# Token lists of experts 1 to 15 by indirect transfers of 8-byte pairs in place of one-hot products

## The chip, the cores and the metric

The kernel runs on one core of one Trainium2 chip. The core has a matrix engine (TensorE, PE in the profile), a vector engine (VectorE, DVE), a scalar engine (ScalarE, ACT), a general engine (GpSimd, POOL) and a queue engine for transfers (SyncE, SP); each runs its own list of instructions and meets the others at semaphores. 16 DMA engines move data between the chip's memory (DRAM) and the core's memories, SBUF (128 partitions) and PSUM (eight banks that TensorE writes to). The metric is the device time of one execution in microseconds (us), the median of several runs.

## What is computed

One layer of an encoder for 2064 tokens (16 learned ones and 2048 of the input) of 1024 channels: a pooling mixer, then a mixture of 16 experts in which each expert picks its 258 tokens itself, then a norm. The part that matters here is the choice of tokens:

```
cap = CAPACITY_FACTOR * T // N_EXPERTS                      # 258
logits = jnp.einsum('btd,de->bte', u, router_w).astype(jnp.float32)
aff = jax.nn.softmax(logits, axis=-1)
g, idx = lax.top_k(jnp.swapaxes(aff, 1, 2), cap)
...
xs = ub[ib]                                                 # the 258 rows of each expert
hid = silu(xs @ w_gate) * (xs @ w_up)
ys = (hid @ w_down) * g
out = zeros((T, D)).at[ib].add(ys)
```

All is float32. Each expert has three weight matrices of 1024 x 2048, 8 MB each.

## The kernel before

**Stages.** First the mixer and the router's logits, 19 tiles of up to 128 tokens (`step` on each engine). Then a search finds, for all experts at once, the affinity that lets 258 tokens pass. `find_slots` turns the choice into a place from 0 to 257 for each chosen token, in the layout of the tokens: partition and tile (`slot`, 128 x 16 experts x 19 tiles); tokens that were not chosen get a place far outside. It runs for expert 0 first, and for experts 1 to 15 after expert 0's list has been read.

**The expert loop.** For each expert `gate_up` makes the hidden values in 32 quarters and `down` the result in 16. A quarter is 24 matmuls of 128 x 128 by 258 columns: each weight block is split into a high and a low part (`w_hi` by ScalarE, `w_lo` by VectorE in `split_rest`), and so are the tokens and the hidden values, and three products of the parts are added for each of 8 blocks. The splits run three quarters ahead of TensorE. SyncE loads pieces of 1 MB into the four slots of `raw`, each as soon as its slot has been split.

**The token list.** A list is needed in another layout than the places are in: place 0 to 127 down the partitions, 128 to 255 likewise, and the last two tokens each repeated for eight chunks of channels. It holds for each place the token's number and its affinity. For the list of expert n+1, made while expert n runs, VectorE compares each of 19 tiles' places (and one empty tile) with the row of all places (`pick`, five tiles in each of the four turns of `gate_up`, L940), which gives one-hot matrices of 128 x 272. Between gate/up and down TensorE multiplies these with `vals`: token number in two parts and affinity in three, all bfloat16 and exact in sum (`make_list`, L1156; three blocks of 19 matmuls of 5 columns, 57 in all). At the first down quarter VectorE copies the finished expert's indices aside (`idx_now`, `gates_now`, `idx_small`) and puts the new list together (`read_list`, L943).

**What follows a list.** GpSimd waits for it (`list_v`), and gathers the 258 rows with three indirect transfers (`gather`, L484) into `x_rows` and `x_left`. TensorE transposes them from the eighth down quarter on. After the expert's end GpSimd adds the weighted results to `h_acc` in DRAM by three indirect transfers (L527 to L531). `carry_wait` is a tiny multiplication on GpSimd that lets the transfers behind it start only after the waits before it.

## Time and profile before

| | |
|---|---|
| median of 3 runs | 2591.71 us (2591.68 to 2593.68) |
| the profiled execution | 2591.47 us |
| its span, first to last instruction | 2589.4 us |
| busy in the span: PE, DVE, ACT, POOL | 96%, 54%, 46%, 7% |
| mean busy share of the 16 DMA engines in the expert loop | 0.60 |
| mixer, router and first list | 0 to 256 us |
| experts | 256 us to the end, some 145 us each |

A row of the timeline gives the start of an instruction, its length, its engine and line, what it writes and reads, and in brackets how long the engine stood idle before it and what released it. Matmuls overlap: each takes about 0.28 us from its start to its end, and the next may start 0.12 us after it. What a matmul adds to the time is the distance between starts. "xN" after a row counts instructions that were merged into it. "issue" in place of a releaser means that the engine waited for nothing that the profile shows.

### The profile page before, as it was taken

How to read it: one execution, taken by the hardware profiler on the slowest of the kernel's cores; microseconds unless marked ns; L12 is line 12 of the kernel's file. 1: busy time of each engine (PE TensorE's matmuls, PEld its weight loads, DVE VectorE, ACT ScalarE, POOL GpSimd, SP SyncE). 2: the span in 40 equal slices, each digit the busy share in tenths (PEclk: the TensorE clock that was granted, in tenths of full speed). 3: DMA queues.
4: the chain of work that ended last, by engine and by line, in shares of the span. 5: the costliest groups of instructions: out<-in, count | busy, mean ns of one | idle time of the engine just before them, and what ended most of it. 6: DMA issues, size and time to landing. Idle time of an engine off the chain costs nothing.

```text
span 2589.4 us, 55918 instructions
## 1 busy us (share of the span) xinstructions
PE 2475.4 (96%) x21150; PEld 2462.9 (95%) x21150; DVE 1397.3 (54%) x2161; ACT 1192.6 (46%) x1765; POOL 193.3 (7%) x190
## 2 busy tenths in 40 slices
PE   7962999999999999999999999999999999999996
PEld 7952999999999999999999999999999999999996
DVE  5556555546454555555454655555454555555474
ACT  5630444444444444444444444444444445444454
POOL 0020001010100001010101001010101001010101
PEclk9975999999999999999999999999999999999998
DMA  7640556665655656565655666666656656566694
GB/s 218 199 147 19 167 194 190 195 178 191 191 185 179 194 195 192 197 178 194 180 188 185 193 194 179 201 184 198 179 179 192 196 186 187 195 181 205 217 316 168
DMA packets 426299, 485.83 MB, mean 188 GB/s; under 512 B 11537, under 2 KB 406529, under 8 KB 426274
## 3 DMA queue, kind: packets, MB, share of 16 engines
q1 hardware_dynamic: 411106, 433.85, 52.4%
q0 software_dynamic: 10560, 34.87, 5.4%
q10 hardware_dynamic: 4608, 16.78, 1.7%
q8 instruction: 16, 0.26, 0.0%
q14 instruction: 9, 0.07, 0.0%
HBM read 443.26 MB, written 42.21 MB: 187 GB/s over the span
## 4 chain that ended last, share of the span: by engine, by line
PE 95%; DVE 2%; issue 1%; DMA 1%; ACT 0%; DVEq 0%; POOL 0%; SPq 0%; POOLq 0%; ACTq 0%
PE bank L1069 92%; PE bank L1074 3%; DVE above L875 0%; DVE above_b L875 0%; DMA nmix<-in_norm_mix 0%; DVE base L882 0%; DMA x_left<-u_rows,idx_chunk 0%; ACT u_t L623 0%; DVE picks L940 0%; DVE pooled_lo L791 0%; DVE pw L818 0%; DVE flips L878 0%; DVE y_rows L1061 0%; ACT junk L719 0%; ACT squares L593 0%
## 5 line engine op out<-in xcount | busy, mean ns | idle before, releaser
L963 DVE TENSOR_TENSOR w_lo<-raw,w_hi 128x1024 fp32r<-128x1024 f32 x765 | 930.1, 1222 | 526.1 <-ACT w_hi L654 524.9
L1069 PE MATMUL bank<-x_hi,w_hi 128*128 128x258 f32 x4096 | 1163.1, 284 | 5.8 <-issue 3.9
L1069 PE MATMUL bank<-x_lo,w_hi 128*128 128x258 f32 x4096 | 1157.5, 283 | 0.0
L1069 PE MATMUL bank<-x_hi,w_lo 128*128 128x258 f32 x4096 | 1153.5, 282 | 0.0
L654 ACT ACTIVATE w_hi<-raw 128x1024 fp32r<-128x1024 f32 x765 | 804.7, 1052 | 271.4 <-PE bank L1069 234.0
L1069 PEld LDWEIGHTS bank<-x_hi,w_hi 128*128 128x128 f32 x4096 | 771.0, 188 | 10.3 <-issue 10.3
L1069 PEld LDWEIGHTS bank<-x_lo,w_hi 128*128 128x128 f32 x4096 | 777.2, 190 | 0.0
L1069 PEld LDWEIGHTS bank<-x_hi,w_lo 128*128 128x128 f32 x4096 | 773.0, 189 | 0.0
L1069 PE MATMUL bank<-hid_hi,w_hi 128*128 128x258 f32 x2048 | 586.6, 286 | 0.0
L1069 PE MATMUL bank<-hid_lo,w_hi 128*128 128x258 f32 x2048 | 579.8, 283 | 0.0
L1069 PE MATMUL bank<-hid_hi,w_lo 128*128 128x258 f32 x2048 | 579.4, 283 | 0.0
L1069 PEld LDWEIGHTS bank<-hid_lo,w_hi 128*128 128x128 f32 x2048 | 388.0, 189 | 0.0
L1069 PEld LDWEIGHTS bank<-hid_hi,w_lo 128*128 128x128 f32 x2048 | 387.3, 189 | 0.0
L1069 PEld LDWEIGHTS bank<-hid_hi,w_hi 128*128 128x128 f32 x2048 | 386.7, 189 | 0.6 <-DVE w_lo L963 0.2
L992 DVE TENSOR_TENSOR hid<-silu,bank 128x258 f32<-128x258 f32 x256 | 108.6, 424 | 505.1 <-PE bank L1069 505.1
L708 ACT ACTIVATE hid_hi<-hid 128x258 f32 (+1 forms) x256 | 107.8, 421 | 458.6 <-DVE hid L992 456.6
L704 ACT ACTIVATE silu<-bank 128x258 f32<-128x258 f32 x256 | 98.9, 386 | 289.0 <-PE bank L1069 289.0
L481 POOL TENSOR_TENSOR carrier<-carrier 128x1 f32<-128x1 f32 x30 | 5.8, 192 | 2003.7 <-DVE gates L958 1338.3
L732 ACT ACTIVATE y_t<-bank 128x258 f32<-128x258 f32 x128 | 49.5, 386 | 201.7 <-PE bank L1069 201.7
L998 DVE TENSOR_TENSOR hid_lo<-hid,hid_hi 128x258 f32 (+1 forms) x256 | 107.8, 421 | 0.0
L940 DVE TENSOR_SCALAR picks<-iota,slot 128x272 bf16 (+1 forms) x320 | 81.8, 288 | 3.3
L528 POOL DMA_INDIRECT h_acc<-y_rows,idx_now x30 | 74.9, 2496 | 12.5 <-issue 12.5
(143 smaller groups left out, 1208.9 us busy)
## 6 DMA issues: line engine op xcount, KB each, us to landing
raw<-in_moe_w_gate SPq DMA_DIRECT2D x128, 1024.0 KB, 5.2
raw<-in_moe_w_up SPq DMA_DIRECT2D x128, 1024.0 KB
raw<-in_moe_w_down SPq DMA_DIRECT2D x128, 1024.0 KB, 4.9
h_in<-in_x SPq DMA_DIRECT2D x18, 512.0 KB, 5.7
x_rows<-h_acc ACTq DMA_DIRECT2D x16, 512.0 KB, 6.0
out<-x_rows ACTq DMA_DIRECT2D x16, 512.0 KB, 4.3
h_acc<-h_mid SPq DMA_DIRECT2D x17, 448.0 KB, 4.9
u_rows<-u_out SPq DMA_DIRECT2D x17, 448.0 KB, 3.0
```

Source lines behind the costliest of these rows:

```text
L481: nc.gpsimd.tensor_tensor(carrier[:, 0:1], carrier[:, 1:2], carrier[:, 1:2], ALU.mult)\
L528: pool.indirect_dma_start(h_acc, bass.IndirectOffsetOnAxis(ap=idx_now[:, b:b + 1], axis=0), y_rows[:, b, :], None, compute_op=ALU.add).the ...
L654: nc.scalar.activation(w_hi[:, a % 4], quarter_view(piece % 4, a % 2), ACT.Copy)\
L704: nc.scalar.activation(silu[:, fc], bank[:, q % 4, 0:CAP], ACT.Silu)\
L708: nc.scalar.activation(hid_hi[:, ds(4 * b + fc, 1)], hid[:, fc % 2:fc % 2 + 1], ACT.Copy).then_inc(hid_hi_done, 1)
L732: nc.scalar.activation(y_t[:, m], bank[:, m % 4, 0:CAP], ACT.Copy).then_inc(y_t_done, 1)
L940: nc.vector.tensor_scalar(picks[:, ds(c0 + c, 1), :], iota[:].unsqueeze(1), src, None, ALU.is_equal).then_inc(picks_done, 1)
L963: nc.vector.tensor_tensor(w_lo[:, a % 4], quarter_view(a // 2 % 4, a % 2), w_hi[:, a % 4].bitcast(f32), ALU.subtract).then_inc(split_lo, 1)
L992: nc.vector.tensor_tensor(hid[:, fc % 2], silu[:, fc], bank[:, q % 4, 0:CAP], ALU.mult).then_inc(hid_done, 1)
L998: nc.vector.tensor_tensor(hid_lo[:, col], hid[:, fc % 2:fc % 2 + 1], hid_hi[:, col].bitcast(f32), ALU.subtract)\
L1069: return nc.tensor.matmul(dst, lhs, rhs, start=start, stop=stop)
L1074: return nc.tensor.matmul(dst, src, ident[0:n, 0:n], is_transpose=True, start=True, stop=True)
```

## The change

Expert 0's list is made as before (`pick`, `make_first_list`, `read_first_list`, now for this expert alone). For the others the one-hot matrices, `pick` in `gate_up` and `make_list` in TensorE's loop are gone, and so are the waits that went with them. In their place:

- `find_slots` for experts 1 to 15 writes places as integers (`slot_rows`); a token that was not chosen gets 4096 plus its partition (`far`, one more column that is loaded at the start). GpSimd keeps a copy of the affinities, turned by expert (`aff_kept`).
- `send_list(n)`, on GpSimd at the head of its loop for expert n, makes the list of expert n+1: it copies the expert's places and affinities aside, issues 19 indirect transfers of 128 pairs (token number, affinity; 8 bytes) to the row `place` of a table of 258 rows in DRAM, where a place over 257 is out of bounds and leaves nothing, waits until all have landed, and reads the table back in the layout of the list by three transfers.
- `read_list` on VectorE waits for that (`list_read`) and makes `idx`, `idx_chunk` and `gates` by three instructions instead of six.

```diff
+            def send_list(n):
+
+                pool.wait_ge(list_copied, 2 * n + 1)
+                nc.gpsimd.tensor_copy(slot_now[:], slot_rows[:, ds(n + 1, 1), :].rearrange("p a c -> p (a c)"))\
+                  .then_inc(list_copied, 1)
+                nc.gpsimd.tensor_copy(pair_now[:, :, 1].bitcast(f32),
+                                      aff_kept[:, ds(n + 1, 1), :].rearrange("p a c -> p (a c)"))\
+                  .then_inc(list_copied, 1)
+                pool.wait_ge(list_copied, 2 * n + 3)
+                pool.wait_ge(carrier_set, 4 * n + 1)
+                carry_wait()
+                for c in range(NT):
+                    pool.indirect_dma_start(list_rows, bass.IndirectOffsetOnAxis(ap=slot_now[:, c:c + 1], axis=0),
+                                            pair_now[:, c, :], None, bounds_check=CAP - 1, oob_is_err=False)\
+                        .then_inc(list_sent, 16)
+                pool.wait_ge(list_sent, 16 * NT * n + 16 * NT)
+                pool.wait_ge(carrier_set, 4 * n + 2)
+                carry_wait()
+                with nc.allow_non_contiguous_dma(reason="a list of pairs"):
+                    pool.dma_start(listed_rows[:, 0:2, :], list_rows[0:256, :].rearrange("(b p) v -> p b v", p=P))\
+                        .then_inc(list_read, 16)
+                    for t in range(LEFT):
+                        pool.dma_start(listed_rows[t:SMALL_ROWS:LEFT, 2, :],
+                                       list_rows[256 + t].partition_broadcast(KD)).then_inc(list_read, 16)
...
             gather()
+            pool.wait_ge(slotted, 1)
+            pool.wait_ge(aff_saved, 1)
             with pool.Fori(0, NE - 1) as n:
-                pool.wait_ge(list_v, LV * n + 2 * LV)
-                pool.wait_ge(carrier_set, 2 * n + 1)
+                send_list(n)
+                pool.wait_ge(list_ready, 3 * n + 6)
+                pool.wait_ge(carrier_set, 4 * n + 3)
                 pool.wait_ge(x_turned, XT * n + XT)
                 carry_wait()
                 gather()
...
+            def read_list(m):
+
+                dve.wait_ge(list_kept, 3 * m)
+                dve.wait_ge(list_read, 16 * READS * m)
+                dve.wait_ge(gathered, 48 * m)
+                nc.vector.tensor_copy(idx[:], listed_rows[:, :, 0]).then_inc(list_ready, 1)
+                nc.vector.scalar_tensor_tensor(out=idx_chunk[:], in0=listed_rows[:, 2, 0:1], scalar=float(KD),
+                                               in1=chunk[:], op0=ALU.mult, op1=ALU.add).then_inc(list_ready, 1)
+                nc.vector.tensor_copy(gates[:], listed_rows[:, :, 1].bitcast(f32)).then_inc(list_ready, 1)
...
-                    if q == 3 and not last:
-                        dve.wait_ge(listed_ps, n + 1)
-                        pick(n + 1, 5 * b)
...
             with pe.Fori(0, NE - 1) as n:
                 with pe.Fori(0, 4) as b:
                     gate_up(n, b)
-                make_list(n + 1, n + 1)
                 for q in range(16):
                     down_quarter(n, q)
```

The order of the instructions on the engines shows where these stand. TensorE at the end of gate/up in the expert loop, before: the last of the 57 small matmuls, and the first down quarter behind them.

```order
L1069 MATMUL bank<-vals,picks 128x5
L1069 ISA
L1069 MATMUL bank<-vals,picks 128x5 x20
L1069 MATMUL bank<-vals,picks 16x5 x19
L1215 ISA
L1216 ISA [waits split_lo]
L1219 REGISTER_ALU [waits hid_lo_done]
L1069 MATMUL bank<-hid_hi,w_hi 128x258 [waits silu_done]
```

The same place after the change:

```order
L1132 MATMUL bank<-x_hi,w_lo 128x258
L1294 REGISTER_ALU
L1294 COMPARE_AND_BRANCH
L1274 ISA
L1275 ISA [waits split_lo]
L1278 REGISTER_ALU [waits hid_lo_done]
L1132 MATMUL bank<-hid_hi,w_hi 128x258 [waits silu_done]
```

The down quarter now follows the last gate/up quarter directly, with the waits that it had. GpSimd at the head of its expert loop, before:

```order
L516 UNCONDITIONAL_BRANCH
L516 ISA
L518 ISA [waits list_v]
L519 ISA [waits carrier_set]
L481 TENSOR_TENSOR carrier<-carrier 128x1 [waits x_turned]
L486 DMA x_rows<-u_rows,idx 128x1024 x2
L489 DMA x_left<-u_rows,idx_chunk 16x128
```

and after the change, from behind the two copies of `send_list` to the carrier ahead of the same gather:

```order
L540 ISA [waits list_copied]
L501 TENSOR_TENSOR carrier<-carrier 128x1 [waits carrier_set]
L543 DMA list_rows<-pair_now,slot_now 258x2 x19
L546 ISA
L547 REGISTER_ALU [waits list_sent]
L501 TENSOR_TENSOR carrier<-carrier 128x1 [waits carrier_set]
L550 DMA listed_rows<-list_rows 128x2x2
L553 DMA listed_rows<-list_rows 8x2 x2
L566 ISA
L567 REGISTER_ALU [waits list_ready]
L568 ISA [waits carrier_set]
L501 TENSOR_TENSOR carrier<-carrier 128x1 [waits x_turned]
```

22 transfers and two waits for transfers now stand ahead of GpSimd's wait for the list. VectorE at the first down quarter, where the list is read, before:

```order
L945 REGISTER_ALU
L946 COPY listed<-bank 128x10 [waits listed_ps]
L948 COPY listed<-bank 16x5
L949 ISA
L950 TENSOR_TENSOR part<-listed 128x3 [waits list_v]
L951 REGISTER_ALU
L952 SCALAR_TENSOR_TENSOR idx<-listed 128x3 [waits gathered]
L955 REGISTER_ALU
L956 SCALAR_TENSOR_TENSOR idx_chunk<-idx,chunk 128x1 [waits list_v]
L958 TENSOR_TENSOR gates<-part,listed 128x3
L962 REGISTER_ALU
L963 TENSOR_TENSOR w_lo<-raw,w_hi 128x1024 [waits split_hi]
```

and after:

```order
L1018 ISA
L1019 REGISTER_ALU [waits list_kept]
L1021 COPY idx<-listed_rows 128x3 [waits gathered,list_read]
L1022 SCALAR_TENSOR_TENSOR idx_chunk<-listed_rows,chunk 128x1
L1024 COPY gates<-listed_rows 128x3
L1028 REGISTER_ALU
L1029 TENSOR_TENSOR w_lo<-raw,w_hi 128x1024 [waits split_hi]
```

The wait for TensorE's product (`listed_ps`) became a wait for transfers (`list_read`), and the same weight split stands behind it.

## Rows read from the trace of the kernel before

**Rows 1.** The page: busy us, share of the span and instructions of each engine.

```profile
PE 2475.4 (96%) x21150; PEld 2462.9 (95%) x21150; DVE 1397.3 (54%) x2161; ACT 1192.6 (46%) x1765; POOL 193.3 (7%) x190
```

**Rows 2.** The page: the chain that ended last, shares of the span by engine.

```profile
PE 95%; DVE 2%; issue 1%; DMA 1%; ACT 0%; DVEq 0%; POOL 0%; SPq 0%; POOLq 0%; ACTq 0%
```

**Rows 3.** Stretches: length, busy us (count) of PE, PEld, DVE, ACT, POOL; clock, DMA, GB/s.

```profile
1000.00:2000.00 1000.00, 998.05 (x8601) 994.94 (x8600) 533.12 (x792) 466.02 (x678) 68.27 (x55) 1.00 0.60 188
```

**Rows 4.** PE's waits by line waited for: us in total, times, longest us.

```profile
PE bank L1074 <- DMA x_left<-u_rows,idx_chunk: 8.8, 1, 8.8
...
PE bank L1069 <- issue: 3.9, 14, 0.3
```

**Rows 5.** Timeline of PE, from gate/up to down of expert 0: start, us, line.

```profile
350.93 1.93 PE L1069 MATMUL bank<-vals,picks 128*128 x57
352.79 0.39 PE L1069 MATMUL bank<-hid_hi,w_hi 128*128 128x258 f32 x1
353.01 0.28 PE L1069 MATMUL bank<-hid_lo,w_hi 128*128 128x258 f32 x1
353.13 0.28 PE L1069 MATMUL bank<-hid_hi,w_lo 128*128 128x258 f32 x1
```

**Rows 6.** The fifteen lists' matmuls on `picks`, summed over fifteen stretches of 10 us.

```profile
sum 150.00, PE 28.91 PEld 26.23 DVE 0.00; mean PE 1.93 PEld 1.75 DVE 0.00
```

**Rows 7.** Timeline of DVE around its first list reading in the loop.

```profile
352.69 0.42 DVE L998 TENSOR_TENSOR hid_lo<-hid,hid_hi 128x258 f32 x1
...
354.54 0.16 DVE L946 COPY listed<-bank 128x10 f32<-128x10 f32 x1
...
355.17 0.15 DVE L958 TENSOR_TENSOR gates<-part,listed 128x3 f32<-128x3 f32 x1
```

**Rows 8.** Timeline of POOL, experts 0 and 1.

```profile
355.59 0.19 POOL L481 TENSOR_TENSOR carrier<-carrier 128x1 f32<-128x1 f32 x1 [108.74 <-DVE gates L958]
...
357.56 1.57 POOL L486 DMA_INDIRECT x_rows<-u_rows,idx  x1 [0.30 <-issue]
...
405.40 2.65 POOL L528 DMA_INDIRECT h_acc<-y_rows,idx_now  x1 [0.53 <-issue]
...
410.99 1.33 POOL L530 DMA_INDIRECT h_acc<-y_small,idx_small  x1 [0.30 <-issue]
500.14 0.19 POOL L481 TENSOR_TENSOR carrier<-carrier 128x1 f32<-128x1 f32 x1 [87.82 <-DVE gates L958]
```

**Rows 9.** The last, bounded scatter (L571): ns min/median/max, starts; and its landing.

```profile
L571 POOL DMA_INDIRECT out<-y_rows,idx_out x3: 893/981/1170, 2575.5 to 2578.3; - x3
...
DMA to landing us min/median/max: 2.5/3.5/3.5
```

**Rows 10.** DMA queues: packets, MB, share of 16 engines; one issue with us to landing.

```profile
q1 hardware_dynamic: 411106, 433.85, 52.4%
q0 software_dynamic: 10560, 34.87, 5.4%
...
h_acc<-y_rows,idx_now POOLq DMA_INDIRECT x30, 9.2
```

**Rows 11.** Timeline of SP, two loads into one slot; and landing of all gate/up pieces.

```profile
414.22 0.37 SPq L440 DMA_DIRECT2D raw<-in_moe_w_gate  x1
...
437.23 0.37 SPq L440 DMA_DIRECT2D raw<-in_moe_w_gate  x1
...
DMA to landing us min/median/max: 5.1/5.2/8.1
```

**Rows 12.** Timelines of the start and of the end of `find_slots` for experts 1 to 15.

```profile
21.34 0.29 POOL L472 CAST tri_b<-cst 128x128 bf16<-128x128 f32 x1 [18.24 <-DMA nfin<-in_norm_final]
...
25.33 1.21 DVE L810 TENSOR_TENSOR h_mid<-bank,h_in 128x1024 f32<-128x1024 f32 x1
...
247.98 0.45 DVE L930 TENSOR_SCALAR slot<-place 128x285 f32<-128x285 f32 x1
```

**Rows 13.** DVE's weight splits in one expert: count, ns min/median/max, starts.

```profile
L963 DVE TENSOR_TENSOR w_lo<-raw,w_hi x33: 1217/1220/1227, 405.3 to 497.7; 128x1024 fp32r<-128x1024 f32 x33
```

More of the change, by code:

```diff
@@ L112, in constants @@
     put("tok_lo", tok % 16)
+    put("tok", tok)
+    put("far", FAR + k)
     low = 4.0 ** np.arange(PAIRS - 1, -1, -1)
@@ L156, in encoder_kernel @@
         iota = sb("iota", [P, PICKED], bf16)
-        slot = sb("slot", [P, NE, 20], f32)
-        vals = sb("vals", [P, NE, 20, 5], bf16)
+        slot = sb("slot", [P, 20], f32)
+        vals = sb("vals", [P, 20, 5], bf16)
+        slot_rows = sb("slot_rows", [P, NE, NT], i32)
+        aff_kept = sb("aff_kept", [P, NE, NT], f32)
+        slot_now = sb("slot_now", [P, NT], i32)
+        pair_now = sb("pair_now", [P, NT, 2], i32)
+        listed_rows = sb("listed_rows", [P, 3, 2], i32)
+        far = sb("far", [P, 1], f32)
         listed = sb("listed", [P, 3, 5], f32)
@@ L392, in _ @@
                 sp.dma_start(chunk[:], consts[:, cols["chunk"][0]:cols["chunk"][1]]).then_inc(loaded_c, 16)
+            with nc.allow_non_contiguous_dma(reason="a column"):
+                sp.dma_start(far[:], consts[:, cols["far"][0]:cols["far"][1]]).then_inc(loaded_c, 16)
             sp.dma_start(reset[:], consts[:, cols["reset"][0]:cols["reset"][1]]).then_inc(loaded_c, 16)
@@ L1165, in make_list @@
                     for c in range(NT):
[L1166 removed]
+                        if b == 0 and c % 5 == 0:
                             pe.wait_ge(picks_done, c + 5)
[L1168 to L1169 removed]
+                        last = mm(bank[0:n, 6, 5 * b:5 * b + 5], picks[:, c, s0:s0 + n], vals[:, c, :],
+                                  c == 0, c == NT - 1)
                 last.then_inc(listed_ps, 1)
             def turn_pair(i, m):
[L1174 to L1175 removed]
+                if i == 2 and isinstance(m, int):
+                    pe.wait_ge(list_v, 2)
                 for k in (2 * i, 2 * i + 1):
```

96 lines of the change are left out of this document (52 added, 44 removed).

## The prediction

> **What bounds the kernel now.** I read the page's table of busy time first: TensorE is busy 96% of the span, VectorE 54%, ScalarE 46% and GpSimd 7% [rows 1]. A busy share alone says little for pipelined matmuls, so next the chain that ended last: TensorE holds 95% of it [rows 2]. Then the stretches: from 1000 to 2000 us TensorE is busy 998.05 of 1000 us at a granted clock of 1.00, while the DMA engines are at 0.60 [rows 3]. Last TensorE's waits: in the fifteen experts it waits for nobody. What that view names lies in the router and at the first list, but for the fourteen loop edges between experts, 0.3 us each [rows 4]. So in the expert loop the time is the sum of TensorE's steps. What is taken out of that sum is gained in full, and what other engines do costs nothing until TensorE begins to wait.
>
> **The change part by part.**
>
> *TensorE, removed.* Between the last gate/up quarter and the first down quarter of each of 15 experts stand 57 matmuls of `make_list`. Their busy time, 28.91 us summed over 15 windows [rows 6], counts the overlap with the following step, so I take start to start: 350.93 to 352.79, 1.86 us, and the same at all experts, since the sum is 15 times 1.93. The first down step after them takes 0.22 (352.79 to 353.01), where the next takes 0.12 [rows 5]. Inside the gate/up stage there is no such long step at a quarter's edge, so I book the extra 0.10 as a consequence of the small matmuls too. Per expert 1.96 us, for 15 experts 29.4 us; without the 0.10 it is 27.9. I take 29.4, since the quarters on the two sides are of one kind, and keep 27.9 for the range.
>
> Does anything become late when the down stage starts 1.96 us earlier? Its first two quarters need weights that VectorE has long split. Its third begins 2 x 24 x 0.12 = 5.76 us after 350.93, at 356.7, and needs all of hid_lo, which ends at 352.69 + 0.42 = 353.1 [rows 5, 7]. So no wait takes the place of the matmuls.
>
> *VectorE, removed.* 20 comparisons in each of 15 experts, and half of the list's reading (six small instructions become three). VectorE waits for ScalarE and TensorE in that stage and TensorE never for it, so this is worth nothing.
>
> *GpSimd, added.* For each list: two small copies, two carriers, 19 indirect transfers, a wait until they landed, three plain transfers that read the list back. All of it lies on an engine that idles 87.82 us at a stretch [rows 8], and is hidden if the list is in SBUF when VectorE asks. The budget: GpSimd is free at 410.99 + 1.33 = 412.3. VectorE's next list reading starts 0.8 us before 500.14 (354.54 to 355.32 is its length) [rows 7, 8], and 1.96 earlier after the change: 497.4. That leaves 85.1 us. VectorE then has some patience: behind the reading stands the split for the fifth down quarter, which begins at 350.93 + 4 x 2.88 = 362.4; less 1.22 for the split and 0.8 for the reading the list may come at 360.4, 5.9 us after VectorE asked at 354.5. Together 91.0 us.
>
> The need, between the cheapest and the dearest rows of the same kind. An indirect transfer of 128 rows costs GpSimd 0.89 when it is a bounded scatter to DRAM [rows 9], 1.57 for a gather and 2.65 for a scatter that adds [rows 8], and 0.30 to the next: 19 x 1.19 = 22.6 to 19 x 2.95 = 56.1 us. Landing takes 2.5 [rows 9] to 9.2 us [rows 10], and once more for the reading. The three plain transfers have no row; as 1.19 to 2.95 each they are 3.6 to 8.9. Copies and carriers I take as four times a carrier with its gap, 0.19 + 0.53 [rows 8]: 2.9. Sum: 34 to 86 us. I take about 40, since the bounded scatter is the same form of instruction. Even the dear end fits into 91.0. The first list has more room: its slots are ready at 247.98 + 0.45 = 248.4 [rows 12] and VectorE asks at 354.5.
>
> Who is queued behind it: on GpSimd only the gather of the same expert, which needs the list anyway; the scatter-add of the finished expert comes later still. On VectorE the weight splits stand behind the new wait for `list_read`, which is where a late list would reach TensorE.
>
> *DMA, added.* Up to 19 x 128 = 2432 packets of 8 bytes per list, of which 258 are in bounds; whether the others move anything no row shows. The weights' queue takes 52.4% of 16 engines' span for 411106 packets, 53 ns each; the software queue 5.4% for 10560, 212 ns each [rows 10]. So a list costs 0 (dropped) to 8 us at the one price and 32 us at the other, of all 16 engines, within some 143 us that leave 40% free [rows 3]. A weight slot is loaded every 437.23 - 414.22 = 23.0 us; less two quarters of reading, 5.8, there are 17.2 us from issue to need, against a landing of 5.2, at most 8.1 [rows 11]. Slack 9 to 12 us. If the queues take turns, the weights get half of the engines where they need 0.60, for at most 64 us: 6 us behind, inside the slack. I take nothing.
>
> *The start.* One more small load (`far`) delays the constants by about 0.5 us; they are in by 21.3, and VectorE first waits for them after the instruction at 25.33 [rows 12]. Nothing. Shorter fills of `vals` lie under the threshold search. Nothing.
>
> *The sum.* Profiled execution 2591.47 us (span 2589.4 and 2.07 around it); less 29.4 is 2562.1. The median of the three runs, 2591.71, stands 0.24 above the profiled one, well within what is left open here.
>
> **A rule that speaks against it.** What the rows show: VectorE's splits run at 1217 to 1227 ns in the expert where GpSimd issues its scatter-adds [rows 13], and the gather at 357.56 took 1.57 beside a split [rows 8]. The Trainium skill, SBUF — State Buffer, under "A bandwidth-pool intuition that's wrong", says that a DMA issued from GpSimd takes about 620 ns alone and about 3100 ns beside a VectorE copy, since GpSimd can't write its descriptors while VectorE holds the port that the two share. By that figure the sum would be an estimate of 19 x 3.4 = 65 us, some 4 us too late with all else at the dear end, and the time about 2615. The same page, under "Who interferes with whom", has an operation on two SBUF tensors, as the split is, take only the read side of that port; the rows above agree in that neither engine is stretched fivefold. Rival 1 has the same mechanism at the prices of rows.
>
> **The rivals.**
>
> *1. The list is late (slower).* Place: VectorE's wait for `list_read` at the first down quarter. It decides from (91.0 - 30.2) / 19 = 3.2 us per transfer, gap included, if all the rest is dear (2.9 + 9.2 + 8.9 + 9.2 = 30.2), and from 4.2 if it is cheap (11.5). Price, with the dearest row and a whole split of 1.22 in front of each: 2.65 + 1.22 + 0.30 = 4.17, 79.2 + 30.2 = 109.4, 18.4 late in 14 experts: 258 us, time 2820. For it: no row has 19 such transfers in a row. Against it: the bounded scatter at 0.89 to 1.17.
>
> *2. Weight pieces are late.* If the small packets go ahead of the weights rather than in turn with them, a part of 32 us falls on one slot. One us beyond the slack per expert gives 15 back: 2577. For it: the software queue's 212 ns per packet; against it: those are packets of kilobytes.
>
> *3. The change doesn't do what it says.* If the small matmuls only filled a wait, the first down quarter would start when hid_lo is done, at 353.1, and the time would stay 2591. Against it: the first down quarter needs only the first eight of the sixteen, and the third quarter starts after 353.1 by itself.
>
> **How the numbers follow.** Forecast 2562.1 with 84%; its own range 2560 to 2565, from 27.9 at one end and a little more than 29.4 at the other. Rival 1: 8%, of which 3 are for GpSimd being held behind VectorE. Rival 2: 5%, from 2566 to 2600, mostly below. Rival 3: 3%. A measurement of this kernel can tell about 0.2%, 5 us, from no change. Faster by more than that: 84 and most of rival 2, 87%. Within it: 5%. Slower: 8%. The range 2559 to 2570 holds the forecast with its bounds and the small end of rival 2.
>
> **What would show it.** TensorE's matmuls on `vals` and `picks` are left at the first list alone, and a down stage follows gate/up with a step of 0.12. The period of an expert, by GpSimd's carriers 500.14 - 355.59 = 144.55 [rows 8], falls to 142.6. GpSimd shows 19 transfers at 0.9 to 1.6 us and then idles until VectorE's gates are set: if instead VectorE's first list copy waits for a DMA, rival 1 holds. ScalarE waits for `raw` DMAs: rival 2. What would make the prediction wrong altogether is a cost of TensorE's own, such as another granted clock than 1.00 in the loop, for which no row gives a reason.

## The result, and the profile after

The changed kernel takes 2761.57 us (median of 4 runs, 2759.86 to 2764.64) against 2591.69 for the kernel before in the same session: 1.066 times as long, 95% interval 1.064 to 1.067. The forecast was 2562.1, a gain; the kernel got slower, and lies 199 us over the forecast. Its profiled execution spans 2759.3 us.

The list was not late, the weights were not late, and TensorE did lose the small matmuls. The first three views, in the order of the prediction, already show where the time went. The page's busy times (us, share of the span, instructions), which answer to [rows 1]:

```profile
PE 2539.8 (92%) x20295; PEld 2498.7 (91%) x20295; DVE 1330.5 (48%) x1816; ACT 1191.7 (43%) x1765; POOL 549.0 (20%) x583
```

TensorE has 855 matmuls fewer (15 x 57) and is yet busy for longer. The stretch of [rows 3], and three shorter ones of the expert that starts at about 557 us (length, busy us and counts of PE, PEld, DVE, ACT, POOL; granted clock, DMA share, GB/s):

```profile
1000.00:2000.00 1000.00, 942.25 (x7461) 926.54 (x7459) 453.85 (x573) 423.80 (x619) 225.30 (x225) 0.95 0.56 171
555.00:574.00 19.00, 18.75 (x159) 18.47 (x158) 8.48 (x11) 10.29 (x16) 13.19 (x12) 1.00 0.75 188
576.00:595.00 19.00, 8.91 (x32) 6.93 (x33) 0.15 (x1) 1.33 (x2) 13.81 (x16) 0.59 0.11 29
601.00:640.00 39.00, 39.00 (x326) 39.00 (x325) 19.97 (x25) 18.39 (x27) 0.00 (x0) 1.00 0.59 189
```

From 576 to 595 TensorE does 32 matmuls where 159 fit; VectorE does one instruction, ScalarE two, the DMA engines rest, and GpSimd alone works. The granted clock, 1.00 on both sides, is 0.59 in between: TensorE's pauses begin at 576, and by 580 the clock is at its lower level (1.2 of 2.4 GHz), where it stays to the end of the pauses and nearly until 600. Three pieces of two us:

```profile
576.00:578.00 2.00, 1.03 (x7) 0.94 (x8) 0.00 (x0) 0.00 (x0) 1.52 (x2) 1.00 0.37 110
...
580.00:582.00 2.00, 1.33 (x5) 1.24 (x6) 0.00 (x0) 0.81 (x2) 1.39 (x3) 0.50 0.02 1
...
600.00:602.00 2.00, 2.00 (x19) 2.00 (x18) 0.42 (x2) 1.33 (x2) 0.00 (x0) 1.00 0.82 261
```

The stretch falls into the one in which GpSimd sends the list: the first of the list's transfers starts at 567.40, the last ends at 591.96 and has landed by 593.2, and TensorE's pauses run from 576 to 594.7. GpSimd's timeline (start, length, line; the idle time before and what ended it), first the list sent during expert 1, then the one during expert 2:

```profile
425.62 1.07 POOL L543 DMA_INDIRECT list_rows<-pair_now,slot_now  x1 [0.15 <-issue]
427.00 2.07 POOL L543 DMA_INDIRECT list_rows<-pair_now,slot_now  x1 [0.30 <-issue]
429.37 1.30 POOL L543 DMA_INDIRECT list_rows<-pair_now,slot_now  x1 [0.30 <-issue]
430.98 1.85 POOL L543 DMA_INDIRECT list_rows<-pair_now,slot_now  x1 [0.30 <-issue]
...
455.96 0.99 POOL L543 DMA_INDIRECT list_rows<-pair_now,slot_now  x1 [0.30 <-issue]
...
461.28 1.07 POOL L553 DMA_DIRECT2D listed_rows<-list_rows  x2
510.67 1.02 POOL L501 TENSOR_TENSOR carrier<-carrier 128x1 f32<-128x1 f32 x1 [48.33 <-DVE gates L1024]
...
567.40 1.06 POOL L543 DMA_INDIRECT list_rows<-pair_now,slot_now  x1 [0.15 <-issue]
568.77 1.01 POOL L543 DMA_INDIRECT list_rows<-pair_now,slot_now  x1 [0.30 <-issue]
...
589.70 0.98 POOL L543 DMA_INDIRECT list_rows<-pair_now,slot_now  x1 [0.30 <-issue]
590.98 0.98 POOL L543 DMA_INDIRECT list_rows<-pair_now,slot_now  x1 [0.30 <-issue]
```

Both lists are early: in expert 1 GpSimd then idles 48.33 us until VectorE has read it. What differs is the length of the transfers. In expert 1 ten of the nineteen take 1.26 to 2.07 us, each of them beside one of VectorE's splits, and nothing is lost: its period is 141.8 us, 2.8 under that of the kernel before. In expert 2 all take 0.98 to 1.17 and follow each other 1.28 to 1.47 apart, and TensorE stops. (In this kernel no transfer that is clear of VectorE's work takes over 1.07 us. Not every one beside a split is stretched: the one at 568.77 is not.) Experts 1 and 4 are of the first kind, the other thirteen of the second. Measured from its first matmul to the first of what follows, the gate/up stage takes 91.42 us in experts 1 and 4 (92.16 before) and 106.7 to 110.0 in the others.

What TensorE waits for there. Its waits (us in total, times, longest), answering to [rows 4], where this was 3.9 us:

```profile
PE bank L1132 <- issue: 109.4, 170, 1.8
```

and a piece of its timeline in expert 2, matmuls first, then weight loads:

```profile
586.55 0.42 PE L1132 MATMUL bank<-x_hi,w_lo 128*128 128x258 f32 x1
586.89 0.38 PE L1132 MATMUL bank<-x_hi,w_hi 128*128 128x258 f32 x1
589.00 0.37 PE L1132 MATMUL bank<-x_lo,w_hi 128*128 128x258 f32 x1 [1.74 <-issue]
```

```profile
586.55 0.34 PEld L1132 LDWEIGHTS bank<-x_hi,w_hi 128*128 128x128 f32 x1
588.29 0.29 PEld L1132 LDWEIGHTS bank<-x_lo,w_hi 128*128 128x128 f32 x1 [1.40 <-issue]
```

"issue" means that nothing in the trace released it. These matmuls are in the middle of a quarter, where the program has no wait, and the weight load itself comes late, so it is not a matmul that waits for its weights. One to four matmuls come, then 0.3 to 2.1 us pass to the start of the next, about one group per GpSimd transfer. ScalarE and VectorE stand still too. ACT's timeline, the last matmul of TensorE's seventh quarter, and DVE's timeline:

```profile
571.81 0.39 ACT L753 ACTIVATE silu<-bank 128x258 f32<-128x258 f32 x1 [1.47 <-PE bank L1132]
...
581.19 0.39 ACT L753 ACTIVATE silu<-bank 128x258 f32<-128x258 f32 x1 [8.05 <-issue]
```

```profile
579.02 0.28 PE L1132 MATMUL bank<-x_hi,w_lo 128*128 128x258 f32 x1 [0.79 <-issue]
```

```profile
573.18 1.22 DVE L1029 TENSOR_TENSOR w_lo<-raw,w_hi 128x1024 fp32r<-128x1024 f32 x1 [1.58 <-issue]
594.85 0.42 DVE L1058 TENSOR_TENSOR hid<-silu,bank 128x258 f32<-128x258 f32 x1 [20.45 <-remote]
595.19 1.22 DVE L1029 TENSOR_TENSOR w_lo<-raw,w_hi 128x1024 fp32r<-128x1024 f32 x1
```

ScalarE's second `silu` of that turn follows the first after one quarter, 2.85 us, when nothing is wrong; that would be 574.7, ahead of TensorE's first pause (576), and it starts at 581.19. This looks as if ScalarE stopped by itself, and first. It did not: `silu` and `hid` wait for TensorE's count of finished quarters (the semaphore `quarters`), and that count comes late. The last matmul of the seventh quarter starts at 579.02, and TensorE goes on with the eighth; the `hid` that needs the seventh starts at 594.85. "remote" means that a semaphore moved then although no instruction of this trace ended; "issue" at 581.19 means here that the event is not on record, as the trace has only 30 of the 32 counts of this expert's gate/up stage. In the kernel before, each count comes 0.3 us after the start of the quarter's last matmul. In e2 below, whose trace has every count, the latest comes 8.4 to 12.8 us after it in each of thirteen experts, and every `silu` of these starts within 0.15 us of its count, as before the change. As the ends of matmuls are modelled, the trace does not tell whether the quarter itself ended late or only its count was late.

The late count costs TensorE time by itself. Its tenth quarter needs the split at 595.19, which stands behind that `hid`; undisturbed the quarter would start at 556.6 + 9 x 2.86 = 582.3. So some 14 of the 18.6 us that this expert loses would be lost even if TensorE did not pause. While VectorE waits, its splits do not hold GpSimd back either: the transfers stay at their shortest until the list is out.

The sum agrees: the excess of the gate/up stages over 91.42 us is 200 us in twelve experts, and 12 in expert 0 over its stage in the kernel before (94.9); 212 in all, and 2761.6 - 212 = 2549, which is what the first experiment gives. The view of waits names 109 us of it; the rest is matmuls that start 0.21 us apart at the lower clock (589.17 to 589.38) in place of 0.12, and pauses that this view counts short or not at all.

### The profile page after: what moved, and what is told of

Read it like the earlier page. It is cut to its first block, busy times and chain, and to the rows that moved or that the text cites. A ratio compares the mean times of both kernels' runs of the same rounds, so it can differ in the third digit from the quotient of the medians.

```text
span 2759.3 us, 53642 instructions
## 1 busy us (share of the span) xinstructions
PE 2539.8 (92%) x20295; PEld 2498.7 (91%) x20295; DVE 1330.5 (48%) x1816; ACT 1191.7 (43%) x1765; POOL 549.0 (20%) x583
## 3 DMA queue, kind: packets, MB, share of 16 engines
q0 software_dynamic: 21120, 35.08, 5.3%
## 4 chain that ended last, share of the span: by engine, by line
PE 92%; issue 5%; DVE 2%; ACT 0%; DMA 0%; DVEq 0%; POOL 0%; SPq 0%; ACTq 0%; POOLq 0%
PE bank L1132 89%; PE bank L1137 3%; DVE above L924 0%; DVE above_b L924 0%; DMA nmix<-in_norm_mix 0%; DVE base L931 0%; DMA x_left<-u_rows,idx_chunk 0%; ACT u_t L672 0%; DVE picks L995 0%; DVE pooled_lo L840 0%; DVE pw L867 0%; DVE flips L927 0%; DVE y_rows L1124 0%; ACT junk L768 0%; ACT squares L642 0%
## 5 line engine op out<-in xcount | busy, mean ns | idle before, releaser
L1132 PE MATMUL bank<-x_lo,w_hi 128*128 128x258 f32 x4096 | 1182.0, 289 | 45.9 <-issue 44.9
L1132 PE MATMUL bank<-x_hi,w_hi 128*128 128x258 f32 x4096 | 1182.3, 289 | 38.6 <-issue 35.3
L1132 PE MATMUL bank<-x_hi,w_lo 128*128 128x258 f32 x4096 | 1181.2, 288 | 30.4 <-issue 29.2
L1132 PEld LDWEIGHTS bank<-x_lo,w_hi 128*128 128x128 f32 x4096 | 794.7, 194 | 56.7 <-issue 56.0
L1132 PEld LDWEIGHTS bank<-x_hi,w_lo 128*128 128x128 f32 x4096 | 796.2, 194 | 48.5 <-issue 48.2
L1132 PEld LDWEIGHTS bank<-x_hi,w_hi 128*128 128x128 f32 x4096 | 795.0, 194 | 45.3 <-issue 44.6
L501 POOL TENSOR_TENSOR carrier<-carrier 128x1 f32<-128x1 f32 x60 | 37.5, 625 | 1723.2 <-DVE gates L1024 1058.8
L543 POOL DMA_INDIRECT list_rows<-pair_now,slot_now x285 | 305.6, 1072 | 85.7 <-issue 84.1
```

The source lines that it names most:

```text
L501: nc.gpsimd.tensor_tensor(carrier[:, 0:1], carrier[:, 1:2], carrier[:, 1:2], ALU.mult)\
L543: pool.indirect_dma_start(list_rows, bass.IndirectOffsetOnAxis(ap=slot_now[:, c:c + 1], axis=0), pair_now[:, c, :], None, bounds_check=CAP ...
L1132: return nc.tensor.matmul(dst, lhs, rhs, start=start, stop=stop)
```

## Experiments

**Theory:** indirect transfers that GpSimd sends back to back stop the other engines; the expectations say "starve", since I took the engines to be left without instructions. **Rivals:** TensorE's own changed program (shorter loop, tiles at other bytes); the reading back; the small writes in DRAM; a GpSimd that is merely busy; the backward branch of TensorE's gate/up loop; the place of the transfers in the expert.

The diffs below are cut to the lines that carry the change, without declarations, waits and semaphore counts; where runs share a block, a comment names the run. Stages and lists are measured in each run's profiled execution.

### e1: the list sent once

```diff
+            fill_table(0)
             with pool.Fori(0, NE - 1) as n:
                 send_list(n)
```

`fill_table` is the two copies and the 19 transfers, taken out of `send_list`, which keeps the carriers, the wait and the three reading transfers.

> The changed kernel, but the 19 transfers of a list are sent once, ahead of the expert loop; every expert from 1 on reads back that one list of expert 1 (its output is therefore that of a kernel that routes 14 experts alike). The three plain GpSimd transfers that read the list back, the waits and both programs of TensorE and VectorE are as in the changed kernel. Theory (the run of GpSimd's transfers starves TensorE): the 13 disturbed experts become like experts 1 and 4, whose period is 141.8 us; 2591.5 - 15 x 2.8 = 2549 us, 2545 to 2556. Rival (TensorE's own program, its shorter loop or the new tile addresses, does it): near 2760. Rival (the reading back does it): near 2760 too, with the stand-still of TensorE at the reading back alone.

2549.23 us, ratio 0.984 (0.983 to 0.986). TensorE's pauses are gone, but for four of 1.7 us in all beside the one list that is sent, ahead of the loop:

```profile
PE bank L1136 <- issue: 5.2, 18, 0.7
```

TensorE's program, the tiles' places and the reading back are those of the changed kernel, so these rivals fall. It is also what the change would bring without its side effect.

### e2, e10, e11, e12, e15: what it is in the transfers

All five are the kernel before, with all its work, and something added to GpSimd at the place where the changed kernel sends its list.

```diff
             with pool.Fori(0, NE - 1) as n:
+                for c in range(NT):      # e2; e10: spot[0:64], pair[0:64]
+                    pool.indirect_dma_start(spare_rows, IndirectOffsetOnAxis(ap=spot[:, c:c + 1], axis=0),
+                                            pair[:], None, bounds_check=NT * P - 1, oob_is_err=False)
+                for c in range(26):      # e11
+                    nc.gpsimd.tensor_tensor(busy_out[:], busy_in[:], busy_in[:], ALU.mult)
+                for c in range(NT):      # e12
+                    pool.dma_start(spare_rows[c * P:(c + 1) * P, :], pair[:])
+                for c in range(NT):      # e15
+                    pool.indirect_dma_start(fetched[:, c, :], None, spare_rows,
+                                            IndirectOffsetOnAxis(ap=spot[:, c:c + 1], axis=0))
```

> The kernel before, all of its work kept, and on GpSimd at the place where the changed kernel sends a list 19 indirect transfers per expert to a spare table, every index out of bounds, so that no pair is written. Theory (the run of GpSimd's transfers starves TensorE, whatever they carry): some 13 of 15 experts get 15 to 19 us longer, 2591.5 + about 200 = 2750 to 2850. Rival (the 258 small writes of a list in DRAM do it): 2591, within 5. Rival (TensorE's changed program does it): 2591, within 5.

> The kernel of e2 with 64 indices per transfer in place of 128, all out of bounds. Undisturbed it is 2592 + 15 = 2607, since gate/up quarters take 2.91 at this place of x_hi. Theory A (what each transfer writes into its queue fills it, so half the rows are half the load): no stand-still, 2600 to 2615. Theory B (the number of transfers per time, not their rows): 15 stand-stills as in e2, 2780 to 2830.

> The kernel before with 26 GpSimd multiplications of 128x304 numbers per expert at the place of e2's transfers, about 1 us each, some 26 us in all, and no transfer. Theory (the transfers do it): no stand-still; 2607 by the place of x_hi, 2600 to 2620, with something more where GpSimd and VectorE stretch each other. Rival (a GpSimd that is busy without a break does it): 15 stand-stills, 2750 or more.

> The kernel of e2 with 19 plain GpSimd transfers of 128 pairs of 8 bytes to a spare table, at addresses known to the program, in place of the indirect ones; all pairs are written. Undisturbed 2607. Theory A (a dense run of GpSimd transfers of any kind does it): stand-stills in most experts, 2700 or more. Theory B (only indirect transfers, which read indices and make each row's address on the fly): 2600 to 2615.

> The kernel before with 19 indirect gathers of 128 pairs of 8 bytes from a spare table into SBUF per expert, at the place of e2's transfers, in place of scatters to it. Undisturbed 2607. Theory (any indirect GpSimd transfer, issued back to back, starves TensorE): as e2, 2700 to 2850. Rival (the scatter form with its bound, whose indices are compared, does it): 2600 to 2615.

Measured: e2 2816.65 us (ratio 1.085 to 1.088), e10 2850.40 (1.098 to 1.102), e15 2833.51 (1.090 to 1.097): in each TensorE stops in all fifteen experts. e11 2605.03 (1.003 to 1.007) and e12 2604.57 (1.003 to 1.006): no pause, and no more than the 2607 that the place of `x_hi` accounts for. TensorE's waits on "issue", in the order e2, e10, e15, e11, e12:

```profile
PE bank L1093 <- issue: 104.1, 205, 2.2
```

```profile
PE bank L1093 <- issue: 129.9, 212, 2.0
```

```profile
PE bank L1099 <- issue: 123.2, 204, 1.7
```

```profile
PE bank L1095 <- issue: 3.5, 14, 0.3
```

```profile
PE bank L1092 <- issue: 3.5, 14, 0.3
```

And GpSimd's own groups in e2, e10, e11 and e12 (count, busy us, mean ns, idle before):

```profile
L538 POOL DMA_INDIRECT spare_rows<-pair,spot x285 | 292.8, 1027 | 84.7 <-issue 84.7
```

```profile
L538 POOL DMA_INDIRECT spare_rows<-pair,spot x285 | 284.2, 997 | 84.7 <-issue 84.7
```

```profile
L542 POOL TENSOR_TENSOR busy_out<-busy_in 128x304 f32<-128x304 f32 x390 | 413.3, 1060 | 29.4
```

```profile
L539 POOL DMA_DIRECT2D spare_rows<-pair x285 | 158.8, 948 | 0.0
```

What is written does not matter (e2 writes no pair at all), nor do the rows of a transfer: with 64 in place of 128 it takes 997 ns in place of 1027, they follow each other faster, and the loss is larger; theory A of e10 falls. Reading is as bad as writing, so the bound is not it. A GpSimd that computes for 27 us on end does nothing to TensorE, and neither do 19 plain transfers which leave GpSimd faster than the indirect ones (fourteen of them in 7.78 us) and do write their pairs. So it is the indirect form, as far as runs of 19 go: the plain run is over after some 10.6 us, about when the stops begin in the others, and a plain run of 25 us was not tried.

### e3, e5, e8, e9, e14: the same list, spread or moved

All five are the changed kernel, and compute what it computes. `pace` is a one-column GpSimd instruction behind a wait.

```diff
                 for c in range(NT):
+                    pace(NT * n + c, quarters, QE * n + c + 1)              # e3, e5: one a quarter
+                    if c % 2 == 0:                                          # e14: two
+                        pace(10 * n + c // 2, quarters, QE * n + c // 2 + 1)
                     pool.indirect_dma_start(list_rows, ...)
+                    pace(NT * n + c, loaded_pool, 16)                       # e9: a wait long met
```

e8 has one `pace` ahead of the loop, on `QE * n + 10` quarters. In e3 the new column stands right behind `listed` and shifts `x_hi` by 32 bytes; in the others it stands behind all tiles.

> The changed kernel, but each of the 19 transfers waits (by a one-column GpSimd instruction) for one more of TensorE's quarters, so that they go out 2.9 us apart over 55 us rather than back to back in 25 to 37; the list is then in SBUF some 60 us into the 92 us of gate/up, early enough. Theory (it is the dense run of transfers that starves TensorE): no stand-stills, 15 x 2.8 under the kernel before: 2549, 2545 to 2560. Rival (each transfer costs TensorE something, dense or not): 13 x 17 us spread over 266 transfers is 0.8 us each, and the time stays near 2760. Rival (the branch of TensorE's loop of four turns, at 22.9 and 45.9 us, falls into a transfer and sets it off): as before between 2560 and 2760, with the stand-stills beginning at a branch.

> The kernel of e3 (one transfer per quarter of TensorE), with the one added column allocated behind all other tiles, so that every tile of the changed kernel stands at the byte where it stood there; in e3 x_hi and what follows it stood 32 bytes higher, and every gate/up quarter took 2.91 us against 2.85 in the changed kernel's undisturbed experts and 2.88 before. Theory (the place of the tiles sets the quarter's length, and pacing costs nothing): 2571.2 - 0.06 x 32 quarters x 16 experts = 2571.2 - 27 to 31, that is 2540 to 2549, and not over 2552. Rival (the paced transfers cost TensorE 1.7 us per expert): 2571 as e3.

> The changed kernel, but the 19 transfers start when TensorE has done 10 quarters, 28.7 us into the expert, behind the first backward branch of the gate/up loop (22.9 us) and ahead of the second (45.9). They take 25 us back to back. Theory A (a dense run starves TensorE after some 8 transfers): first stand-still at about 38 us, 13 us or more lost per expert, 2740 or more. Theory B (the branch): first stand-still at 41.5 to 46.5 us, and the loss is what is left of the run by then, 7 to 12 us of transfers, about half of the changed kernel's: 2600 to 2680. Theory C (only the run right at the start of an expert does it): 2549.

> The changed kernel, with a one-column GpSimd instruction behind each of the 19 transfers, whose wait has long been met: the transfers go out some 2.0 us apart (1.28 and about 0.7) in place of 1.28, at the same start, 10.8 us into the expert, and TensorE is not waited for. Theory (it is the density of the transfers: stand-stills came at a mean spacing of 1.3 to 1.4 us over the first nine, none where VectorE's splits stretched it to 1.65 and more, and none in e8 at 1.68): no stand-still, 2549, 2544 to 2556. Rival (the place near the start of the expert, which e8 and e5 moved away from, does it): stand-stills at 18 to 24 us as in the changed kernel, 2700 or more.

> The kernel of e5 with two transfers per quarter in place of one: two go out 1.3 us apart, then GpSimd waits for TensorE's next quarter, so the mean is 1.44 us, with a rest of 1.6 us after each pair. Theory (the mean spacing over some nine transfers decides, border between 1.4 and 1.65): stand-stills in some experts, but short ones, since a TensorE that stands still holds the next pair back: 2555 to 2640. Rival (a rest after two transfers is enough): 2549, 2544 to 2556.

Measured: e3 2571.19 us (ratio 0.990 to 0.994), e5 2550.72 (0.982 to 0.985), e8 2549.34 (0.982 to 0.986), e9 2558.18 (0.986 to 0.991), e14 2553.86 (0.983 to 0.988). In e3, e5, e8 and e9 TensorE never pauses; in e14 it does so three times, see below. The stretch of [rows 3] in e8:

```profile
1000.00:2000.00 1000.00, 998.33 (x8360) 996.35 (x8360) 513.81 (x651) 474.86 (x690) 265.32 (x250) 1.00 0.64 192
```

e5 and e8 are faster than both kernels. (e3 lies 11 us over its range; its gate/up stages take 93.1 us. e5 and e9 lie 2 us over theirs; 7 and 6 of experts 1 to 14 run at the longer of two gate/up stages, see e6.) e8 says more than its place: its transfers cover both the branch at 45.7 us and TensorE's run-up to it, back to back, and nothing happens, so the branch is not the trigger. But "back to back" is not as dense there as it sounds:

```profile
714.04 1.05 POOL L552 DMA_INDIRECT list_rows<-pair_now,slot_now  x1 [0.57 <-issue]
715.40 1.01 POOL L552 DMA_INDIRECT list_rows<-pair_now,slot_now  x1 [0.30 <-issue]
716.71 1.97 POOL L552 DMA_INDIRECT list_rows<-pair_now,slot_now  x1 [0.30 <-issue]
718.99 0.98 POOL L552 DMA_INDIRECT list_rows<-pair_now,slot_now  x1 [0.30 <-issue]
```

Starting 29.7 us into the expert, seven of the nineteen take 1.26 to 1.97 us, beside a split, as in expert 1 of the changed kernel. Theory C of e8, that only the start of an expert is exposed, is what e9 answers: at the old start, spread, nothing stops either.

e14 was meant at 1.44 us and came out at 1.6 to 1.7, since the added instructions cost GpSimd more than I took. It shows something of the border all the same: in two of its lists TensorE pauses in the middle of a quarter, twice behind the eighteenth transfer (1.0 us in all) and once behind the nineteenth (0.3 us). These are the short stops in some experts that its theory expected; its time lies just under that theory's range and inside the rival's. Its waits, and the first of the three pauses:

```profile
PE bank L1142 <- issue: 5.0, 17, 0.6
...
868.49 0.39 PE L1142 MATMUL bank<-x_lo,w_hi 128*128 128x258 f32 x1 [0.42 <-issue]
```

In e9 TensorE does not pause, but its counts come late already. The last matmul of the thirteenth quarter of expert 1, and the `silu` that waits for that quarter:

```profile
436.60 0.28 PE L1142 MATMUL bank<-x_hi,w_lo 128*128 128x258 f32 x1
```

```profile
438.97 0.39 ACT L763 ACTIVATE silu<-bank 128x258 f32<-128x258 f32 x1 [2.93 <-remote]
```

That is 2.37 us from start to start, where e8 has 0.31. TensorE did not wait for it, as those engines run ahead.

### e7, e13: the rivals of place, and spacing by itself

```diff
                 gather()                      # e7: e2's loop stands here, beside the down stage
                 for c in range(NT):
                     pool.indirect_dma_start(spare_rows, ...)
+                    nc.gpsimd.tensor_tensor(busy_out[:], busy_in[:], busy_in[:], ALU.mult)   # e13: 128x128, e2's place
```

> The kernel of e2 (the kernel before with 19 out-of-bounds transfers per expert), but the transfers stand behind the gather of the next rows, beside the down stage, where TensorE's program runs 49 us without a backward branch. As in e2 x_hi stands 160 bytes higher than before, gate/up quarters 2.91, so undisturbed it is 2592 + 15. Theory A (a dense run starves TensorE wherever it lies, after some 8 transfers): 15 x 13 to 19 us more, 2790 to 2850. Theory B (the run must cover a backward branch of TensorE's loop): no stand-still, 2600 to 2615.

> The kernel of e2 with one GpSimd multiplication of 128x128 numbers (about 0.4 us) behind each of the 19 out-of-bounds transfers, so that they go out some 1.6 to 1.9 us apart; same place, nothing waits for another engine. Undisturbed 2607. Theory (spacing alone decides: stand-stills at 1.2 to 1.4 us, none at 1.65 and more): 2600 to 2615, or a stand-still in a few experts if the spacing stays under 1.6. Rival (19 indirect transfers of an expert cost TensorE 17 us however they are spaced within it): 2780 or more.

e7: 2729.87 us (ratio 1.049 to 1.057), stops in 14 of 15 experts, beginning 117 to 119 us into the expert, in the straight part of TensorE's program. The loss is 5 to 13 us each, less than I expected. e13: 2604.72 (1.004 to 1.008), none. Two TensorE waits of e7 (quarters, then transposes), and GpSimd's groups in e13:

```profile
PE bank L1093 <- issue: 49.2, 100, 1.1
PE bank L1098 <- issue: 11.2, 28, 0.8
```

```profile
L542 POOL DMA_INDIRECT spare_rows<-pair,spot x285 | 363.0, 1274 | 46.8 <-issue 46.8
L546 POOL TENSOR_TENSOR busy_out<-busy_in 128x128 f32<-128x128 f32 x285 | 146.1, 512 | 7.5
```

So neither the place nor the branch decides; the same 285 transfers do no harm when half a microsecond of GpSimd's own work lies between them, which puts them some 2.05 us apart.

### e4: an attempt on the branch that showed something else

```diff
-                with pe.Fori(0, 4) as b:
-                    gate_up(n, b)
+                with pe.Fori(0, 2) as b:
+                    gate_up(n, 2 * b)
+                    gate_up(n, 2 * b + 1)
```

> The changed kernel, but TensorE's gate/up loop runs two turns of sixteen quarters in place of four of eight, so that its first backward branch comes at 45.9 us, when the list has been sent, and not at 22.9. Theory that the branch during the sends is the trigger: no stand-still in any expert, 2549 to 2560. Theory that the dense run of transfers alone does it: still 2700 to 2800, with the first stand-still 18 to 24 us into the expert as it is now.

2685.91 us (ratio 1.028 to 1.045; its two runs, 2667.37 and 2704.44, lie 37 us apart), neither of the two. In the profiled one five experts stop, ten don't, and at each loop edge between experts TensorE now stands 3.4 to 3.7 us. The longer loop no longer stays loaded: the queue of instruction pages, in the changed kernel and in e4 (packets, MB, share), and the edge ahead of expert 2:

```profile
q8 instruction: 16, 0.26, 0.0%
```

```profile
q8 instruction: 143, 2.34, 0.4%
```

```profile
564.72 0.57 PE L1132 MATMUL bank<-x_hi,w_hi 128*128 128x258 f32 x1 [3.39 <-issue]
```

I take it that the pause moves the expert's start against VectorE's splits and so thins the transfers. e4 is no clean test of the branch; e7 and e8 are.

### All lists together

Time from the start of a list's first transfer to the start of its tenth (nine steps), by whether TensorE paused beside the list without a wait that the profile shows:

| kernel | stopped: lists, us | not stopped: lists, us |
|---|---|---|
| changed kernel | 13, 11.8 to 12.8 | 2, 14.4 to 15.1 |
| e1 (its one list) | 1, 12.3 | 0 |
| e2, e10, e15 | 45, 11.1 to 13.0 | 0 |
| e4 | 5, 11.7 to 13.6 | 10, 13.9 to 15.0 |
| e7 | 14, 12.6 to 12.8 | 1, 14.2 |
| e14 | 2, 14.5 to 14.7 | 13, 13.7 to 15.3 |
| e8, e9 | 0 | 30, 14.0 to 18.3 |
| e3, e5, e13 | 0 | 45, 16.3 to 26.2 |

Of 181 lists all 78 that took up to 13.6 us (1.51 a step) stopped TensorE, and of the 103 from 13.7 on only the two of e14 did, late and briefly. The border is softer than that sounds: three lists of e4, at 13.0 to 13.6, cost only 1.7 us of pauses each. A part of what sharpness there is is feedback, since a waiting VectorE lets the later transfers through faster; over the first seven transfers, nearly all ahead of the first stop, the stopped lists took 7.4 to 8.9 us (9.8 and 10.4 in e14) and the others 8.5 to 17.5. The first pause comes after six to twelve transfers, in e1's list and one of e10 after sixteen, in e14 after eighteen and nineteen.

### e6: the place of `x_hi`

Without the pauses the change gives 2549 where the prediction's terms give 2562. I took tiles that moved to be the cause of the rest.

```diff
+        spacer = sb("spacer", [P, 32], f32)
         idx = sb("idx", [P, 3], i32)
```

> The kernel before with an unused tile of 128 bytes per partition in front of idx, so that x_hi, x_lo and the hid tiles stand 128 bytes higher, at the same byte modulo 512 as in the changed kernel; nothing else is changed. Theory (the gain beyond the small matmuls that e1 shows, 2562 - 2549, is the place of x_hi): gate/up quarters of 2.85 us, 0.74 x 16 + 0.14 x 15 = 14 less: 2576 to 2581. Rival (that gain comes from the change itself): 2592, within 3.

2590.47 us, ratio 0.998 to 1.000: no difference, and the expectation was wrong as it stood. In its trace the gate/up stage takes 91.42 us in eight of the sixteen experts and 92.68 in the other eight, where the kernel before takes 92.16 in each of experts 1 to 15. With the tiles 32 bytes higher still, in e3, it is 93.1 in experts 1 to 14. So the place of the tiles does set the length of a quarter (2.85, 2.88 or 2.91 us), but at the changed kernel's place there are two levels, and what picks one is open: of experts 1 to 14, 12 are at the lower in e1, 8 in e9 and 7 in e6.

## Why the prediction was wrong

**The terms that held.** *The small matmuls.* Between e6 and e1, which have the tiles at the same bytes, the period of an expert differs by 143.8 - 141.8 = 2.0 us at the lower level and 145.0 - 143.1 = 1.9 at the upper; the forecast was 1.96. Nothing is late at the third down quarter. *GpSimd's need.* From the first copy (423.34) to the landing of the last reading transfer (465.6) it takes 42.2 us in expert 1; I had taken about 40, between 34 and 86, and 0.98 to 2.07 per transfer lies between the two ends. The budget of 85 us was 0.3 too large (the reading starts 1.05 us ahead of the carrier [rows 7, 8], not 0.8), and was not needed: GpSimd idles 47.9 us and more until VectorE has read the list. *DMA.* The software queue's packets double to 21120 and its share stays at 5.3%, and VectorE and ScalarE never wait for a piece of weights. So rivals 1, 2 and 3 are all refuted.

**The step that failed** is in the first part, where the reading of the profile is turned into a rule: "What is taken out of that sum is gained in full, and what other engines do costs nothing until TensorE begins to wait." From there on GpSimd's 19 transfers were followed only through the queues that the program shows: who stands behind them on GpSimd, on VectorE, on the DMA engines. What GpSimd does to the engines beside it had no term: it stood at nothing, and the runs show 12 to 19 us of TensorE for each of thirteen of the fifteen lists, 212 us in all. The prediction named "a cost of TensorE's own, such as another granted clock than 1.00" as what would make it wrong altogether and set it aside, as no row gave a reason. No row could: the longest run of indirect transfers in the trace of before is three, and the stops begin after six or more. I wrote of rival 1 that no row has 19 such transfers in a row, and drew from it a doubt about the length of one transfer alone. The bound from both sides that I put on each transfer's price on GpSimd should have been put on its price for TensorE too, and the range should have held it.

The range was also too narrow on its good side. Without the stops the kernel takes 2549, 13 under the forecast: the quarters run at 2.85 us in most experts in place of 2.88, about 0.74 us per expert. The change moves the tiles, which I did not look at; but e6, with the tiles at the same place, runs only half of its experts at 2.85 and gains nothing, so why most experts of e1 and e8 do is open.

**The figure of the Trainium skill that I weighed** (SBUF — State Buffer, "A bandwidth-pool intuition that's wrong") did not appear. The Trainium skill has it for a VectorE copy; beside the split, which reads two tiles, transfers stretch from 0.98 to at most 2.07 us, not fivefold. And the stretching that I feared goes with the lists that do no harm, in experts 1 and 4 and in all of e8; that a thinner run is enough, e13 shows.

**What is shown and what is not.** Shown: a run of indirect GpSimd transfers that start 1.2 to 1.5 us apart makes TensorE pause in the middle of quarters, after six to twelve of them in most lists, while nothing in the trace holds it; and it makes TensorE's counts of finished quarters late, for which ScalarE and VectorE then wait. Plain transfers (19 of them) and computing do neither. The same transfers at 1.52 us and more cost TensorE 1.0 us of pauses at most, in two lists of 103. Not shown: why. That TensorE lacks instructions would fit pauses in the middle of a quarter and late weight loads, but not a count that comes late for matmuls that were started. The Trainium skill, Runtime: NRT & Kernel Launch, under "Instruction fetch mechanics", says that an engine fetches its instructions by itself, page by page, mostly hidden, and pays where a branch leaves the pages it holds. e4 agrees with the second part (143 page packets, 3.4 us at an edge). The first does not cover the stops of the changed kernel, whose page queue moves the same 16 packets as before, none of them between 404 and 2600 us. Nor is it tested whether the recording takes part: no run shows the stops without a recorded trace, and the changed kernel's trace lacks 25 of 768 of TensorE's counts (that of e2, which stops as well, lacks none).

## What to carry to other kernels

A run of indirect GpSimd transfers is not free because GpSimd idles: keep it to a few at a time (three in a row stop nothing in the kernel before), or spread it (in e5 one per quarter of TensorE, by a wait on the busiest engine's progress, which also stops the run if that engine stops), and it is hidden indeed: 2550.7 us, 1.7% under the kernel before. When a change puts much more of an operation on an idle engine than any row has in a row, make that one of the cases that the range must hold. And where an engine pauses with "issue", look at what its neighbours do in that stretch before looking at its own program, and compare the start of each waiting instruction with the end of the work that it waits for: "issue" and "remote" can hide a semaphore that moved late.

## What the runs showed of the hardware that was not expected

- Indirect transfers 1.2 to 1.5 us apart stop TensorE, mostly after six to twelve of them, and its count for a finished quarter comes up to 12.8 us after the quarter's last matmul started (e2; 0.3 before). ScalarE and VectorE wait for that count, VectorE then no longer slows GpSimd, and TensorE's clock falls to its lower level (0.50), so that a list of 25 us costs 12 to 19 us of TensorE.
- An indirect transfer costs GpSimd nearly the same with 64 rows as with 128 (997 and 1027 ns), and with all rows out of bounds as in the lists, where 258 of 2432 are in bounds (1027 and 1072); a plain one of 128 rows follows the last after 0.56 us.
- A gate/up quarter of 24 matmuls takes 2.88 us in the kernel before, 2.85 or 2.90 with the tiles behind one point 128 bytes higher (e6), and 2.91 with them 32 bytes higher still (e3 against e5). Which of the moved tiles does it was not separated.
- TensorE's loop over an expert stays loaded with eight gate/up quarters in its inner turn (no instruction page moves between 404 and 2600 us), and is fetched again for every expert with sixteen (e4), for 3.4 to 3.7 us at each edge.
